# MLP results gathered without the norm's scale, additions of VectorE and ScalarE reordered, and layer two's x added in the last group

## What is computed

```python
def rmsnorm(x, g, eps=NORM_EPS):
    y = x32 * lax.rsqrt(jnp.mean(x32 * x32, axis=-1, keepdims=True) + eps)
    return y * g

def sq_relu_mlp(h, w1, w2):
    u = jax.nn.relu(h @ w1)
    return (u * u) @ w2

x = x + sq_relu_mlp(rmsnorm(x, mlp_norm[l]), mlp_w1[l], mlp_w2[l])
```

## Time and profile before

| what | value |
|---|---|
| median of 3 runs | 1066.61 us |
| lowest and highest | 1066.57, 1066.99 us |
| profiled execution, its own time | 1068.11 us |
| span of its trace | 1066.3 us |
| TensorE's mean granted clock | 0.994 |

### The profile page before, as it was taken

One profiled execution on the slowest core, in us unless ns is written; L12 is line 12 of the kernel. 1 busy time (PEld: TensorE's weight loads), 2 busy tenths in 40 slices (PEclk: granted clock), 3 DMA queues, 4 the chain that ended last, 5 costly groups with the idle time before them and its releaser, 6 DMA issues.

```text
span 1066.3 us, 15296 instructions
## 1 busy us (share of the span) xinstructions
PE 1035.3 (97%) x5920; PEld 884.0 (83%) x5920; DVE 814.2 (76%) x1157; ACT 647.0 (61%) x940; POOL 106.2 (10%) x133
## 2 busy tenths in 40 slices
PE   8999999999999999999999999999999999999996
PEld 5777889879979979978877777778979979978975
DVE  7889876885896886898656666566797697698697
ACT  6699865645745645655436656566764664664665
POOL 1000021220101101100000000012011011011012
PEclk9999999999999999999999999999999999999998
DMA  7222289598598598562421111257689589679672
GB/s 262 81 79 96 80 210 247 119 239 219 116 253 220 113 257 216 114 171 72 126 60 60 60 60 40 61 189 158 187 183 233 176 173 230 190 161 241 190 155 102
DMA packets 47592, 165.29 MB, mean 155 GB/s; under 512 B 5408, under 2 KB 5536, under 8 KB 47392
## 3 DMA queue, kind: packets, MB, share of 16 engines
q1 hardware_dynamic: 31536, 109.59, 30.6%
q0 software_dynamic: 15552, 53.48, 27.5%
q10 hardware_dynamic: 432, 1.24, 0.3%
HBM read 159.05 MB, written 2.10 MB: 151 GB/s over the span
## 4 chain that ended last, share of the span: by engine, by line
PE 68%; DVE 14%; issue 7%; DMA 6%; ACT 4%; POOL 1%; SPq 0%; DVEq 0%; POOLq 0%; ACTq 0%
PE ps L1832 21%; PE ps L1965 19%; PE ps L2000 16%; DVE w_lo L1120 5%; PE ps L2063 4%; DMA q<-weights 3%; PE ps L2122 2%; DMA w_raw<-weights 2%; ACT w_hi L618 2%; DVE r L1460 2%; PE ps L2148 2%; PE ps L1891 1%; DVE value L1498 1%; PE ps L2137 1%; DVE a_lo L1487 1%
## 5 line engine op out<-in xcount | busy, mean ns | idle before, releaser
L1965 PE MATMUL ps<-x_hi,w_hi 128*128 128x256 f32 x896 | 254.9, 284 | 2.5 <-DVE w_lo L1120 1.8
L1965 PE MATMUL ps<-x_hi,w_lo 128*128 128x256 f32 x896 | 254.3, 284 | 0.0
L1965 PE MATMUL ps<-x_lo,w_hi 128*128 128x256 f32 x896 | 254.2, 284 | 0.0
L1120 DVE TENSOR_TENSOR w_lo<-w_raw,w_hi 128x1024 fp32r<-128x1024 f32 x134 | 163.7, 1222 | 81.5 <-ACT w_hi L618 81.1
L618 ACT ACTIVATE w_hi<-w_raw 128x1024 fp32r<-128x1024 f32 x134 | 141.4, 1055 | 136.5 <-DMA w_raw<-weights 88.7
L1120 DVE TENSOR_TENSOR w_lo<-q,w_hi 128x1024 fp32r<-128x1024 f32 x144 | 177.0, 1230 | 58.7 <-ACT w_hi L618 57.9
L618 ACT ACTIVATE w_hi<-q 128x1024 fp32r<-128x1024 f32 x144 | 151.6, 1053 | 107.8 <-PE ps L1965 45.4
L2000 PE MATMUL ps<-w_hi,a_hi 128*128 128x512 f32 x448 | 177.1, 395 | 14.3 <-DVE value L1498 12.4
L1965 PEld LDWEIGHTS ps<-x_hi,w_hi 128*128 128x128 f32 x896 | 172.7, 193 | 3.4 <-DVE w_lo L1120 2.0
L2000 PE MATMUL ps<-w_hi,a_lo 128*128 128x512 f32 x448 | 175.2, 391 | 0.0
L2000 PE MATMUL ps<-w_lo,a_hi 128*128 128x512 f32 x448 | 175.2, 391 | 0.0
(11 more groups left out here) (218 smaller groups left out, 1651.2 us busy)
## 6 DMA issues: line engine op xcount, KB each, us to landing
w_raw<-weights SPq DMA_DIRECT2D x134, 512.0 KB, 4.3
q<-weights POOLq DMA_DIRECT2D x96, 512.0 KB, 8.3
q<-weights SPq DMA_DIRECT2D x64, 512.0 KB, 4.7
x<-x_t SPq DMA_DIRECT2D x8, 256.0 KB, 6.0
y_t<-value SPq DMA_DIRECT2D x8, 256.0 KB, 2.3
acc<-work POOLq DMA_DIRECT2D x6, 256.0 KB, 3.3
rstd<-work POOLq DMA_DIRECT2D x6, 256.0 KB, 5.1
w_raw<-weights SPq DMA_DIRECT2D x4, 256.0 KB, 4.8
```

The source lines that it names most:

```text
L1120: nc.vector.tensor_tensor(w_lo[:, t % RING, :], src, w_hi[:, t % RING, :], ALU.subtract).then_inc(wlo_done, 1)
L1965: ins = nc.tensor.matmul(to, w[:, t % RING, ws], o[:, op, j, :], start=fresh and j == 0 and f % 2 == 0 and n == 0, stop=j == PAIRS - 1 and ...
```

## The change

In all groups but the last of a layer, `add_product` no longer applies `scale2`: one operation of 128x1024 takes both banks, a plain copy where y is fresh (now in group 0 of both layers) and an addition elsewhere. In the last group ScalarE first multiplies y by `scale2` in place (`scaled_result`, eight operations of 128x512, two at each of s = 1 to 4), after product 6 of the group before has been added, and the last group's own products are added with the scale as before. TensorE's `turn_x` go from group (1,0) to group (1,3), and VectorE's `add_turned` adds x from PSUM to the scaled y there; `turned_rows` falls away.

VectorE's order is written out step by step. Product 1 is added right behind product 0, ahead of the split at s = 16; products 2 to 5 are added behind the splits of s = 18, 21, 23 and 25, and a_lo 4 moves to after s = 19. ScalarE's a_hi 4 and 5 move from s = 17 and 19 to 19 and 20. In `residual_step` the split of the MLP's tile 3 moves ahead of the last sums: ahead of `sums_hi` on ScalarE, and on VectorE ahead of x_lo of the sums and of the first quarter sum. TensorE's wait for `scale_done` falls away, and VectorE's in group 0 gives way to one for `y_times_scale` in the last group.

```diff
@@ ScalarE: residual_step, scaled_result, mlp
                     if m == NCH - 1:
+                        split_hi(t + m + RING)
                         sums_hi(j)
-                        split_hi(t + m + RING)
...
-            def turned_rows(n):
-                for f in (2 * n, 2 * n + 1):
-                    act.wait_ge(turned, NCH + f + 1)
...
+            def scaled_result(layer, f):
+                tok, half = divmod(f, 2)
+                if f == 0:
+                    act.wait_ge(scale_done, layer + 1)
+                    act.wait_ge(y_read, sums_read(layer, GROUPS - 2, NPROD - 1))
+                to = y[:, tok, HALVES[half]]
+                nc.scalar.activation(to, to, ACT.Copy, scale=scale2[:, half, tok:tok + 1]).then_inc(y_times_scale, 1)
...
-                    if (layer, g) == (1, 0) and s in (2, 4, 6, 8):
-                        turned_rows(s // 2 - 1)
+                    if g == GROUPS - 1 and 1 <= s <= 4:
+                        scaled_result(layer, 2 * s - 2)
+                        scaled_result(layer, 2 * s - 1)
...
-                    for i, at in enumerate((9, 13, 14, 15, 17, 19, 21)):
+                    for i, at in enumerate((9, 13, 14, 15, 19, 20, 21)):
@@ VectorE: residual_step
                 lo_of(PAIRS - 1, H21)
+                split_lo(t + NCH - 1 + RING)
                 lo_of(PAIRS - 1, T1)
@@ VectorE: add_product, add_turned
-                add_bank(layer, g, i, 0)
-                add_bank(layer, g, i, 1).then_inc(y_read, 1)
+                if g == GROUPS - 1:
+                    add_bank(layer, g, i, 0)
+                    add_bank(layer, g, i, 1).then_inc(y_read, 1)
+                    return
+                tokens, half = DOWN[i]
+                to = y[:, 2 * tokens:2 * tokens + 2, HALVES[half]]
+                banks = ps[:, BANKS_SUM[i % 2][0]:BANKS_SUM[i % 2][1] + 1, :]
+                if g == 0 and i in FIRST_SUM:
+                    ins = nc.vector.tensor_copy(to, banks)
+                else:
+                    ins = nc.vector.tensor_tensor(to, to, banks, ALU.add)
+                ins.then_inc(y_read, 1)
+
+            def add_turned(f):
+                tok, half = divmod(f, 2)
+                dve.wait_ge(turned, NCH + f + 1)
+                dve.wait_ge(y_times_scale, 2 * QB + f + 1)
+                to = y[:, tok, HALVES[half]]
+                nc.vector.tensor_tensor(to, to, ps[:, BANKS_TURN[f % 2], :], ALU.add).then_inc(turned_read, 1)
@@ VectorE: mlp, written out; the steps before s = 8, and those from s = 14
+                quarter_sum(layer, g, 0, 0)
+                if g:
+                    split(0)
+                quarter_sum(layer, g, 0, 1)
+                if g:
+                    add_product(layer, g - 1, NPROD - 1)
+                for s in range(1, 8):
+                    if (layer, g) == (1, GROUPS - 1) and s in (3, 5, 7):
+                        add_turned(s - 3)
+                        add_turned(s - 2)
+                    split(s)
...
+                act_lo(layer, g, 2)
+                act_sum(layer, g, 3)
+                split(15)
+                if g == GROUPS - 1:
+                    dve.wait_ge(y_times_scale, 2 * QB * (layer + 1))
+                if (layer, g) == (1, GROUPS - 1):
+                    dve.wait_ge(turned_read, 2 * QB)
+                add_product(layer, g, 0)
+                add_product(layer, g, 1)
+                split(16)
+                act_lo(layer, g, 3)
+                split(17)
+                act_sum(layer, g, 4)
+                split(18)
+                add_product(layer, g, 2)
+                split(19)
+                act_lo(layer, g, 4)
+                split(20)
+                act_lo(layer, g, 5)
+                split(21)
+                add_product(layer, g, 3)
+                split(22)
+                act_lo(layer, g, 6)
+                split(23)
+                add_product(layer, g, 4)
+                split(24)
+                split(25)
+                add_product(layer, g, 5)
+                split(26)
+                split(27)
@@ TensorE
-                    if (layer, g) == (1, 0) and i < 4:
+                    if (layer, g) == (1, GROUPS - 1) and i < 4:
                         turn_x(2 * i)
                         turn_x(2 * i + 1)
...
                 if f == 0:
-                    pe.wait_ge(bank_read, B_MLP1)
+                    pe.wait_ge(y_read, sums_read(1, GROUPS - 2, NPROD - 1))
...
-                            elif i == 1:
-                                pe.wait_ge(scale_done, layer + 1)
-                            if (layer, g, i) == (1, 0, 0):
+                            if (layer, g, i) == (1, GROUPS - 1, 0):
                                 pe.wait_ge(turned_read, 2 * QB)
```

More of the change, by code:

```diff
@@ L366, in build @@
         y_read = sem("y_read")
+        y_times_scale = sem("y_times_scale")
         turned = sem("turned")
@@ L1493, in add_bank @@
                 tok = 2 * tokens + n
-                bank = ps[:, BANKS_SUM[i % 2][n], :]
                 to = y[:, tok, HALVES[half]]
-                if layer == 0 and g == 0 and i in FIRST_SUM:
-                    return nc.vector.tensor_scalar(to, bank, scale2[:, half, tok:tok + 1], None, ALU.mult)
-                return nc.vector.scalar_tensor_tensor(out=to, in0=bank, scalar=scale2[:, half, tok:tok + 1],
+                return nc.vector.scalar_tensor_tensor(out=to, in0=ps[:, BANKS_SUM[i % 2][n], :],
+                                                      scalar=scale2[:, half, tok:tok + 1],
                                                       in1=to, op0=ALU.mult, op1=ALU.add)
@@ L1563, in mlp @@
-                    if after is not None and s == PER - 1:
-                        after(NPROD - 2)
+                up_sum(layer, g, 0)
+                split(8)
+                if (layer, g) == (1, GROUPS - 1):
+                    add_turned(6)
+                    add_turned(7)
+                split(9)
+                up_sum(layer, g, 1)
+                split(10)
+                act_lo(layer, g, 0)
+                split(11)
+                quarter_sum(layer, g, 1, 0)
+                up_sum(layer, g, 2)
@@ new lines, in mlp @@
+                split(12)
+                quarter_sum(layer, g, 1, 1)
+                act_sum(layer, g, 1)
+                split(13)
+                act_lo(layer, g, 1)
+                act_sum(layer, g, 2)
+                split(14)
+                act_lo(layer, g, 2)
[3 more added lines that the diff above has]
+                    dve.wait_ge(y_times_scale, 2 * QB * (layer + 1))
+                if (layer, g) == (1, GROUPS - 1):
+                    dve.wait_ge(turned_read, 2 * QB)
```

47 lines of the change are left out of this document (2 added, 45 removed).

## The result

The changed kernel takes 1059.2 us, the median of five runs (1057.81 to 1064.18), beside 1066.99 us of the kernel before in five runs of the same session (1066.57 to 1067.96): a ratio of 0.9936, 95% interval 0.9911 to 0.9961. That is faster, by 7.8 us where 13.9 was forecast, and above the range of 1048.8 to 1057.8. The profiled execution of the change took 1064.18 us, 5.0 more than its median; its span is 3.9 us shorter than that of before. I therefore profiled the change once more (the first experiment), and read its places in both profiles.

A forecast was written before the change was run, and what follows sets the result against it. TensorE, busy 1035.3 of 1066.3 us, was taken as the bound. Stalls 15.5 + low clock 1.6 - starts and turns 1.7 - new clock drop 1.5 = 13.9 us off 1066.61 gives 1052.7 us, range 1048.8 to 1057.8.

The forecast's parts named there:

- The down stalls: TensorE's waits before product 3 in the down stretches go, with product 1 added right behind product 0: 15.5 us gained.
- the low clock of (0,0): TensorE's reduced clock after the down stall of layer zero's first group goes with that stall: 1.6 us gained.
- the first rival: Smaller down-stretch waits replace the stalls, a_lo 4 or product 1's sum being late: 4 to 6.4 us go back; 17%.
- a_hi 4: Rival at product 4: ScalarE's a_hi 4, behind w_hi 22, is held by a late GpSimd sum; slower, 1076 us; 3%.
- all eight stalls go: Every MLP group's down stretch loses its wait before product 3: 14.2 us of waits plus 1.3 of unnamed gap.
- The merged additions: On VectorE, two scaled half additions become one 128x1024: 7.6 us off VectorE, worth 0 to the kernel's time.
- the scale on ScalarE: Eight in-place activations per layer in the last group, some 5 to 6 us in all, are covered: 0.
- The turned x: Four pairs of turns moved to the up stretch of (1,3) cost 0.8 each on TensorE's path: 3.2 us lost.
- The layers' starts: With tile 3's split earlier and turns moved away, layer one's start gains 1.5 us; layer zero's 0.
- the gate: VectorE's statistics copy, awaited by tile 6 of (1,0), stays at 748.6, between 0.7 earlier and 0.65 later.
- The clock: One drop of TensorE's clock after its wait at tile 6 of (1,0), charged 1.5 us, from 0 to 1.7.
- The rule on the queues: DMA engines take turns between queues, so tile 7's load, sharing with GpSimd's sums, would land 0.6 later: sum 0.6 worse.

The follow-up runs named there:

- the first experiment: The changed kernel again with no edit, for a second profile and as control: 1060.21 us, ratio 0.9909 against the kernel before.
- experiment 10: The change with statistics two steps earlier and turns one product later, plus unscaled additions and copies as two of 128x512: 1052.03 us, ratio 0.9842.
- experiment 6: The change with the four turn pairs of (1,3), and VectorE's additions of x, one up product later: 1057.08 us, ratio 0.9884.
- experiment 5: The change with GpSimd's first two sums of group 0 also waiting for VectorE's quarter sums: 1056.3 us, ratio 0.987.
- experiment 2: The kernel before with only the change's order of VectorE's additions and ScalarE's a_hi: 1053.42 us, ratio 0.9842.
- experiment 3: The change with the split of the MLP's tile 3 put back behind the last sums, as before: 1055.61 us, ratio 0.9871.
- experiment 4: The change with the norm's statistics at s = 2 instead of s = 4 of group 0: 1052.53 us, ratio 0.9847.
- experiment 11: The change without turn_x and add_turned, leaving layer two's x out of the result: 1053.45 us, ratio 0.9867.
- experiment 9: The change with the edits of experiment 4, experiment 5 and experiment 6 together: 1053.35 us, ratio 0.9858.

## Why the prediction was wrong

**The down stalls: right.** Seven of eight went, at 1.61 to 2.21 us each in the profile, and the low clock of (0,0) with its one (3.14; 3.64 in the second profile). In sum 15.1 and 15.5 beside 15.15 forecast for those seven. The addition of product 1 began at D + 11.1, 0.3 sooner than worked out. Products 4 to 6 were not late in these seven, so the first rival did not come, nor did a_hi 4.

**The eighth stall, (1,3) down: -1.95 forecast, -0.1 and -0.8 measured.** The step "all eight stalls go" held for the stall and not for the stretch. In its place come a wait at product 5 and one ahead of product 6, for a w_lo that VectorE reaches late; ScalarE had sat 4.07 us for a load, and from the split behind it (1037.55) VectorE works without a pause up to that w_lo (in the second profile the wait ahead of product 6 alone, 1.1):

```profile
1036.46 1.06 ACT L619 ACTIVATE w_hi<-w_raw 128x1024 fp32r<-128x1024 f32 x1 [4.07 <-DMA w_raw<-weights]
...
1040.24 0.47 PE L2041 MATMUL ps<-w_hi,a_hi 128*128 128x512 f32 x1 [0.28 <-DVE value L1498]
1047.19 0.47 PE L2041 MATMUL ps<-w_hi,a_hi 128*128 128x512 f32 x1 [1.23 <-DVE w_lo L1121]
```

The same stretch takes 38.9 to 40.7 in the other kernels here, whatever their start. What sets it was not tried, and the load is the likely cause, not a shown one.

**The merged additions and the scale on ScalarE: 0, right:** experiment 10 shows no gain from merging, and no wait of TensorE for the scaling stands in the profiles.

**The turned x: 3.2 forecast, 5.05 measured.** The rate was nearly right (0.86 to 0.88 a pair, 0.8 taken). The step that failed is that the first pair was given no wait: "TensorE has no slack there" was said of the pairs, but product 6's sum of the group before, behind w_lo 1 in VectorE's queue, was placed for ScalarE's scaling, at some 5 us into the group where it ended at 7.2, and not checked for the turn, which needs the same sum for its banks. It cost 1.5, and experiment 6 took it away.

**The layers' starts: the step that failed most.** "I take the gate as unchanged at 748.6, between 0.7 earlier and 0.65 later", and for layer zero "0, between 0.7 gained and 0.5 lost". Measured, the gate (the copy of the statistics) came 1.4 and 1.6 us later in (0,0), and 1.0 and 1.5 later in (1,0), from the first up matmul. I had followed the move on VectorE to SyncE's loads, and in (0,0) the shifts were right (0.5 later, 0.8 earlier); in (1,0) they were 1.1 later and 0.2 earlier. What failed is that tile 7's load, on which the gate hangs, was taken to land as before, at worst 0.65 later. It took 10.7 us from its issue in (0,0) (8.4 before) and 10.4 in (1,0) (9.1 before), behind a tile 6 that was late itself. And I had not followed the move on ScalarE, whose last square came 0.7 sooner in (0,0), and with it GpSimd's two sums. Together the two shifts gave the sums 1.3 us more of a lead, and tile 6's load 2.2 us more to land. Experiment 5 shows that without the lead it is 3.2 faster than in the change. The move was followed on SyncE's queue, and GpSimd's was left out. Up to 1 us of the 1.4 in (0,0) may be chance, since two kernels with the old start had the copy there 1.0 later than the profile of before (experiments 2 and 3).

**The clock: foreseen in one place of two, and too small.** A drop after the wait at tile 6 of (1,0) was charged with 1.5 and came, and cost 2.5: from tile 6 on the stretch took 25.7 us in both profiles, where before it took 24.0 with a turn pair of 0.86 in it. Not foreseen was one in (0,0), where the wait grew from 0.6 to 2.0 us; there the rest of the stretch took 24.6 in place of 23.1. So of what the two starts cost beyond the forecast, 2.5 us is the clock and the other half (2.4 and 3.1) the gate. All of it is gone in experiment 4 with the waits. The Trainium skill, "TensorE: Matmul & The Clock Gate", part 1, says that the clock follows how busy the array has recently been, with a varying phase. The runs agree that the length of a wait alone doesn't tell. At tile 6 of (0,0) TensorE waited 2.0 us in the change, and the clock fell to 0.72; it waited 2.03 in experiment 11, and it stayed at 1.00; it waited 1.77 in experiment 6, and it fell (columns as in the earlier trace rows, experiment 11 and then 6):

```profile
176.00:182.00 6.00, 6.00 (x52) 6.00 (x52) 4.25 (x8) 2.73 (x4) 0.00 (x0) 1.00 0.98 331
```

```profile
176.00:182.00 6.00, 6.00 (x42) 6.00 (x42) 3.20 (x3) 1.69 (x2) 0.00 (x0) 0.78 0.87 317
```

**The rule on the queues.** "DMA: Bandwidth & Descriptors", section SWDGE vs HWDGE vs iDMA, of the Trainium skill had let me price 0.6 for tile 7 sharing with GpSimd's sums. The direction agrees: tile 7's load landed 1.4 us later in (0,0) and 1.0 in (1,0), from the first up matmul. But the delay begins with tile 6's load, whose flight differs by 2.2 to 3.2 us in (0,0) with who was issued first (before and experiment 5, beside the change), and for that I had no term.

**The sum.** Misses, as means of the two profiles: (0,0) up 3.0, (1,0) up 2.2, (1,3) up 1.9, (1,3) down 1.5: 8.6 of 13.9, less 0.2 that the other down stretches gave beyond the forecast. That leaves 5.5, and the two profiles show 5.3 and 5.6 from the first up matmul to TensorE's end. The medians show 7.8 and 9.2: the profiled execution of the change was the slowest of its set both times, by 5.0 and 1.9 us above the median (that of before by 1.5), and in the second set the kernel before itself took 2.4 us more. The prediction gave the starts bounds under 1 us, and they came 2.9 and 1.9 us longer than forecast, 3.2 and 2.5 in the second profile: that is where its range was too narrow.

## What to carry to other kernels

When a step is moved in a hand-written order, follow it on every engine that has a half of it, and through each to the transfers that it releases: here a split moved forward to save a wait of 1.8 us let another queue's transfers get ahead of a load, and cost more than the wait. Where a stall ends on a small copy that is queued behind a late operation, move the copy; no cost of that shows here, and it gained more than any shift of the late load. And try the parts of a change alone: the reordering by itself was 6.8 us faster than the whole.

## What the runs showed of the hardware

Three things I had not expected. When the first of two 512 KB accumulating transfers of GpSimd was issued 1.4 us ahead of a 512 KB load of SyncE's queue and the second 0.8 ahead, the load landed in 6.9 us; with the first 0.1 ahead and the second 0.4 behind in 4.7, and with the load 0.5 ahead of the first in 3.7 (layer zero's start in the profiles of after, before and experiment 5; the page's median for such loads is 4.3). Over both layers and all profiles here it is 6.9 to 8.1 us, 4.6 to 4.7, and 3.7 to 4.3 in experiments 5 and 9. A pair of turns of 8 matmuls over 128 columns delays the 256-column stream by 0.86 us. And merging two additions of 128x512 from two banks into one of 128x1024 saves VectorE little when neither carries a scale: one takes 1213 ns and two take 2 x 679, 145 more, in the rows of the change and of experiment 10:

```profile
L1519 DVE TENSOR_TENSOR value<-value,ps 128x512 f32<-128x512 f32 x68 | 43.4, 679 | 1.2 <-PE ps L2045 1.2
```
